# 44 products of the identity with a constant tile, put into the waits of TensorE's queue in the router stage

## What is computed

```python
x = x + g1 * rmsnorm(y, post_mix_gain)                      # y: output projection of the mixer
h = rmsnorm(x, pre_ffn_gain) * (1.0 + sc2) + sh2
gl = h @ w_group + b_group                                  # 256 x 4
el = (h @ w_expert + b_expert).reshape(n, 4, 8)             # 256 x 32, grouped
g_idx = argmax(gl); g_w = softmax(gl)[g_idx]                # one group per token
tv, ti = top_k(softmax(el[rows, g_idx]), 2)                 # two experts inside it
wts = g_w * tv / sum(tv)
for e in range(32):                                         # the expert loop
    out += gates[:, e] * ((silu(h @ wg[e]) * (h @ wu[e])) @ wd[e])
```

## Time and profile before

| | us |
|---|---|
| median of 3 runs (lowest, highest) | 780.46 (779.82, 781.46) |
| the profiled execution, its own time | 777.64 |
| its span, first to last instruction | 775.9 |
| mean granted TensorE clock over the span | 0.974 |
| TensorE busy | 722.6 (93% of the span) |
| VectorE busy | 638.9 (82%) |
| ScalarE busy | 524.9 (68%) |
| GpSimd busy | 314.2 (40%) |

### The profile page before, as it was taken

The page is one execution under the profiler, slowest core; times in us unless marked ns, Lnnn a source line. Parts: engine busy times, 40 slices in busy tenths (PEclk is TensorE's granted clock), DMA queues, the critical chain, the costliest instruction groups (busy, mean ns, idle before and its releaser), DMA issues.

```text
span 775.9 us, 12741 instructions
## 1 busy us (share of the span) xinstructions
PE 722.6 (93%) x4760; PEld 578.9 (75%) x4760; DVE 638.9 (82%) x552; ACT 524.9 (68%) x544; POOL 314.2 (40%) x213
## 2 busy tenths in 40 slices
PE   4899689899589999999999999999999999999994
PEld 4785566444467888888888888888888888888883
DVE  3723584727648999999999999999999999999995
ACT  2200222555627878888887888887888888788873
POOL 5810000030053566654456654456665445665000
PEclk9999999999679999999999999999999999999998
DMA  9999975930548899999999999999999999999901
GB/s 332 398 361 410 386 290 201 337 118 0 217 148 318 308 384 374 383 362 374 377 382 375 367 373 366 377 379 371 378 369 374 365 385 376 376 374 366 356 1 58
DMA packets 101901, 249.20 MB, mean 321 GB/s; under 512 B 7109, under 2 KB 7153, under 8 KB 99825
## 3 DMA queue, kind: packets, MB, share of 16 engines
q1 hardware_dynamic: 97472, 244.33, 85.1%
q10 hardware_dynamic: 3970, 2.94, 1.2%
q0 software_dynamic: 432, 1.59, 0.6%
HBM read 247.78 MB, written 1.07 MB: 321 GB/s over the span
## 4 chain that ended last, share of the span: by engine, by line
PE 83%; DVE 9%; ACTq 2%; DMA 2%; ACT 2%; issue 1%; POOL 0%; DVEq 0%; SPq 0%
PE PS L1359 46%; PE PS L1347 8%; PE PS L1327 7%; PE PS L1318 6%; PE PS L1269 4%; PE PS L1154 3%; DVE MOD L739 2%; DMA W<-in_w_ada_dram 2%; PE PS L1133 2%; PE PS L1148 2%; PE PS L1337 2%; ACTq L552 1%; DVE MOD L755 1%; PE PS L1089 1%; DVE S L833 1%
## 5 line engine op out<-in xcount | busy, mean ns | idle before, releaser
L980 DVE TENSOR_TENSOR WL<-W,WH 128x2048 fp32r<-128x2048 f32 x187 | 419.8, 2295 | 5.3 <-ACT WH L642 5.3
L642 ACT CAST WH<-W 128x2048 fp32r<-128x2048 f32 x187 | 349.6, 1902 | 46.7 <-PE PS L1359 46.7
L434 POOL TENSOR_SCALAR OG<-slot_no,cur 128x128 f32<-128x128 f32 x64 | 161.7, 2531 | 0.0
L1359 PE MATMUL PS<-WH,XT 128*128 128x512 f32 x512 | 139.7, 394 | 0.7 <-DVE XT L999 0.7
L1359 PE MATMUL PS<-WL,XT 128*128 128x512 f32 x508 | 138.3, 394 | 0.0
L421 POOL COPY cur<-PG 128x4 f32 (+1 forms) x33 | 8.3, 251 | 273.0 <-PE PS L1337 225.4
L1359 PEld LDWEIGHTS PS<-WH,XT 128*128 128x128 f32 x512 | 95.9, 188 | 23.4 <-DVE XT L999 0.8
L1359 PEld LDWEIGHTS PS<-WL,XT 128*128 128x128 f32 x508 | 95.4, 188 | 22.0
L431 POOL TENSOR_SCALAR OH<-slot_no,cur 128x128 bf16<-128x128 f32 x64 | 106.5, 1673 | 0.0
L1359 PE MATMUL PS<-WH,HT 128*128 128x512 f32 x248 | 68.4, 398 | 1.5 <-issue 1.5
L1359 PE MATMUL PS<-WL,HT 128*128 128x512 f32 x248 | 68.5, 398 | 0.0
(11 more groups left out here) (206 smaller groups left out, 817.6 us busy)
## 6 DMA issues: line engine op xcount, KB each, us to landing
W<-in_w_gate_dram SPq DMA_DIRECT2D x64, 1024.0 KB, 8.2
W<-in_w_down_dram SPq DMA_DIRECT2D x64, 1024.0 KB, 6.2
W<-in_w_up_dram SPq DMA_DIRECT2D x63, 1024.0 KB, 9.9
W<-in_w_ada_dram SPq DMA_DIRECT2D x24, 1024.0 KB, 11.3
W<-in_w_in_dram SPq DMA_DIRECT2D x12, 1024.0 KB, 16.8
W<-in_w_out_dram SPq DMA_DIRECT2D x4, 1024.0 KB, 8.4
toe<-line_dram POOLq DMA_DIRECT2D x1, 1536.0 KB, 12.8
X<-in_x_dram ACTq DMA_DIRECT2D x1, 1024.0 KB, 10.0
```

Of the source, the lines that this page charges most:

```text
L434: nc.gpsimd.tensor_scalar(OG[:, buf, t, :], slot_no[:], cur[:, buf, 0, t:t + 1], cur[:, buf, 1, t:t + 1], ALU.is_equal, ALU.mult).then_inc ...
L642: nc.scalar.copy(WH[:, (UPE * odd + u) % SPLITS, :], source).then_inc(hi_ready, 1)
L980: nc.vector.tensor_tensor(low, source, WH[:, (UPE * odd + u) % SPLITS, :].bitcast(f32), ALU.subtract).then_inc(lo_ready, 1)
L1359: last = nc.tensor.matmul(PS[:, bank, :], lhsT, w[:, q * 512:(q + 1) * 512], start=begin, stop=end)
```

## The change

A helper `turn_over(n, bank)` is added on PE's queue. It issues n products `ident` x `before` (128 x 128 by 128 columns, float32) into the first 128 columns of a bank. They wait for nothing, raise no semaphore, and nobody reads what they write. They are put at five places: 2 behind the transposes of t = 0, 8 ahead of the transposes of t = 1, 2 behind those, 18 behind the logits ahead of the wait for `routed`, and 14 behind the clearing products ahead of the wait for `placed`. That is 44 products, 88 records. Nothing else is changed.

```diff
+            def turn_over(n, bank):
+
+                for i in range(n):
+                    nc.tensor.matmul(PS[:, bank, 0:P], ident[:], before[:], start=True, stop=True)
+
             pe.wait_ge(router_in, 64)
             for t in range(TT):
+                if t:
+                    turn_over(8, 7)
                 transpose_h(t, 2, 4)
+                turn_over(2, 1 if t else 7)
                 pe.wait_ge(hT_ready, 2 * (t + 1))
...
             last.then_inc(logit_mm, 1)
 
+            turn_over(18, 3)
             pe.wait_ge(routed, 1)
...
                 nc.tensor.matmul(PS[:, 4 + b, :], ident16[:], GU[:, 0:256].bitcast(bf16), start=True, stop=True)
+            turn_over(14, 3)
             pe.wait_ge(placed, 1)
```

## The result

Measured side by side, the kernel with the change takes 775.53 us (median of 8 executions, 772.31 to 776.80), the kernel before 779.85 (8, 777.41 to 781.46): ratio 0.9946, 95% interval 0.9929 to 0.9962. Over all comparisons of this study the median of before is 779.6 (81 executions) and that of the change 775.5 (16): 4.0 us. The profiled execution of the change took 775.41 us, with a span of 773.7.

A forecast was written before the change was run, and what follows sets the result against it. PE was taken to bound the kernel, with the loop at its pace. Gains of 1.54 (logits' copy), 0.15 (places) and 1.15 us (gather) sum to 2.84; 780.46 - 2.84 = 777.6 us, range 775.8 to 780.4.

The forecast's parts named there:

- Bound and mechanism: Whole kernel: PE bounds it, the loop passes on an earlier start, and unbroken products hold the router stage's clock at full.
- What a product costs: Each added product, two records: 0.22 us at the full clock (bound 0.44), 0.43 at half (bound 0.86).
- Covers: PE's idle waits at the five places: each batch fits its wait at the full clock, so each costs 0.
- Case C: Router stage: clock still falls before t = 1, the eighteen end late; 0.7 us won, 779.8 us; chance 0.22.
- Stage: Output projection's end to first expert product: 1.54 + 0.15 + 1.15 = 2.84 us won, 27.3 us where it was 30.1.
- DVE's rests: Ahead of the logits' copy: two DVE instructions end last, at 206.29, so 1.04 us of PE's gain is lost.
- the places: Five products after DVE's chain: about 1 us shorter, but DVE's gate weights limit the gain to 0.15 us.
- rival B: Expert loop's first turn: the low spell at 236.7 to 240.0 goes too, 1.6 us more, 776.0 us; chance 0.13.
- The base: Whole kernel: the 2.84 us sum is taken from the median of the runs, 780.46, not the profiled 777.64.
- The range: Whole kernel's time: 775.8 to 780.4 us, said to hold a little over 8 in 10.
- D: Large batches at half clock: products don't raise it and outlast their waits, +5.7 us, 786.2 us; chance 0.07.
- E: Expert loop: takes the 2.8 us back as a weight transfer is last there; no change, 780.5 us; chance 0.08.

The follow-up runs named there:

- the narrow products: The changed kernel with its 44 products made 4 columns wide in place of 128, at the same places: 785.38 us, ratio 1.0081 to the kernel before.
- the six products in the loop: The kernel before with 6 products added in the expert loop's first turn and nothing in the router stage: 777.65 us, ratio 0.9973.

## Why the prediction was wrong, point by point

- *Bound and mechanism*: right. PE is the chain's main part (83%), the loop passes on what it gets (525.5 to 526.3 us from the third gather to the end in every profile), and the gain is the clock's, as the narrow products show.
- *What a product costs*: right. 0.22 us forecast; 4.29/18 = 0.24 with the last record's tail, and 0.43 to 0.44 at half clock (7.84/18). It is not so that the trace had no float32 product of 128 columns: L1203 has them. Two records from 117.54, at full clock, take 0.38 us together where one takes 0.27, so they start 0.11 us apart, which bears the price out. The rule of the Trainium skill against which the forecast set its rows (TensorE: Matmul & The Clock Gate, Back-to-back issue gap) has 56 ns and 107 ns for a matmul of 128 columns without the load of its stationary operand; the runs show 0.11 to 0.12 and 0.21 to 0.22 us for a record with it. By the rule eighteen products take 3.9 us at half clock, and would have been in time; the eighteen narrow ones took 7.84.
- *Covers*: right for the large batches, at 0. Wrong for the eight: the sum has them at 1.76 us within 2.27. That holds at the full clock alone, and in three of four profiles the clock fell ahead of them or in them; in the first they take 3.44 us and the transposes are 1.1 us late. Case C had this fall, at a chance of 0.22, but put the recovery behind the logits, with the eighteen; it came with the eight themselves or in the transposes. In the first profile transposes and logits ran at full clock (1.04 and 1.98 us), and of C's loss of 1.54 about half happened: the logits' copy came 0.7 us earlier than before, not 1.54.
- *Stage*: 2.84 us forecast, 2.3 to 2.4 measured in the mean, 3.1 where the clock did not fall ahead of the eight; there the logits' copy came 1.8 us earlier, 1.54 forecast. DVE's rests, the places and POOL ended the waits as forecast; only the transposes, held up by the eight, did not.
- *The step that failed* is the one set apart as rival B: "At 236.7 to 240.0 the clock is 0.50 in expert 1, at a cost of half of 3.3 us = 1.6 [...] nothing in the change removes it". The sum has it at nothing. It measured 1.8 us on the mean of the first turn and belongs into the sum. The price was right; the chance of 0.13 was not, as far as four profiles tell, nor was the view that only that spell reaches the loop. In all three profiles of the kernel before the low clock takes something there: in two by the later spell, in one by both that and the first one lasting into expert 0 (25.6 to 27.8 us); with the six products in the loop it was the first one alone. In the change it took nothing in three profiles of four. I had read the end of the first spell at 222.98, just behind the gather, as a fixed point, because the one profile had it so.
- *The base*: setting the sum against the median and not against the profiled execution was right: in a second execution the 2 us by which it was longer lay in the first stage, and in a third, 4 us longer, 2.3 of them in the first turn. But that median was of three runs, 780.46. Side by side with the change the kernel before took 779.85, and 779.6 over 81 executions, so the base was 0.6 to 0.9 us too high. The measured gain of 4.3 taken from 780.46 gives 776.1, which is inside the range.
- *The range*: B gives 776.0, and the low end lay 0.2 us under it, with nothing added for B together with scatter of the base. With the base as measured, B gives 779.85 - 2.84 - 1.6 = 775.4, and 775.53 came out. That this is so close is in part luck: the stage gave some 0.5 us less than its 2.84, and the first turn 0.2 more than 1.6. So the missing term and the base together put the time 0.3 us below the range; neither would have done it alone.
- *The rivals*: D is what the narrow products did. The rule on the order of matmuls named beside it (Trainium skill, TensorE: Matmul & The Clock Gate, The mechanism) agrees with that kernel's trace, where the places start at 216.90, when the last of the eighteen has started. E did not occur.

What decides in a given execution of the change whether the later spell comes is open.

## What to carry to other kernels

Where a stage of small work leaves TensorE at half clock, unread products in its waits can bring it back, if each batch ends before its wait even at half clock, or if the batch itself brings the clock up early enough; products that don't raise it cost the time by which they outlast the waits (6.3 us here). Price a low spell beyond the stage in which it is seen: where it ends differs from one execution to the next, so take several profiles, and sum what it takes from the work behind. A speed-up of one engine is worth what the next queue lets through: 0.7 us of PE's gain at the logits went to two VectorE instructions that stood ahead of their reader.

## What the runs showed of the hardware that I had not expected

- PE counted as busy for 17.57 of 17.60 us in the kernel with products of 4 columns and loads of 128, and the granted clock stayed at 0.50; with the same number of products of 128 columns at the same places it was back at 1.00 3.4 us after it fell (198.2 to 201.6).
- At half clock a product of 4 columns costs as much as one of 128: 18 narrow ones took 7.84 us and 14 took 5.97, 0.43 to 0.44 each; the 8 wide ones in the profile of the change took 3.44, 0.43 each.
- One execution of the same kernel differs from the next in where its low spells begin and end: in three profiles of the kernel before, the stage's spell ended at 222.98, 225.99 and 231.43 us, that is 1.1 us ahead of the first expert product, 0.8 ahead of it, and 4.8 behind it.
